# Hybrid decoder layer: last state product left out, exponential's table called early, output norm's root by Newton steps

## The chip, the cores and the metric

The kernel runs on one core of one Trainium2 chip. The metric is the device time of one execution in microseconds. Engines are TensorE (PE; PEld is its weight loads), VectorE (DVE), ScalarE (ACT), GpSimd (POOL) and SyncE (SP), which issues the weight transfers.

## The reference

One decoder layer over 512 tokens of width 1024, in float32: a SwiGLU half-step, a mixer, a second SwiGLU half-step and a final norm. The mixer projects once and runs two groups. The first is a gated DeltaNet with 4 heads of 128, in 8 chunks of 64 tokens. For each chunk:

```python
def step(state, inp):
    q_c, k_c, u_c, w_c, g_c, qk_c = inp
    v_new = u_c - w_c @ state
    o = (q_c * jnp.exp(g_c)[..., None]) @ state + qk_c @ v_new
    ...
    state = state * jnp.exp(g_last)[..., None, None] + jnp.einsum('bhcd,bhce->bhde', k_dec, v_new)
    return state, o
_, o = lax.scan(step, state0, xs)
...
o = rmsnorm(o, out_norm) * jax.nn.silu(z)
```

The state after the last chunk isn't returned. The norm divides `o` by sqrt(mean(o*o) + 1e-6), one value for each token and head. The second group is attention with 8 query heads of 64 on 2 key heads, in three branches (compressed, selected, window; at this length the selected and the window branch see all earlier keys). Both groups' outputs go through one output projection.

## The kernel before, in words

The first half-step, the projections, the mixer, the output projection and the second half-step follow each other on each engine's own queue; engines meet through semaphores only. In the mixer a list written out by `schedule()` gives all engines one order: 14 half projections, each in three groups of products (lines 592 to 594), between which come the rounds of the DeltaNet (`gdn`, a round is a list of jobs), rotary embedding and the compressed branch; then the attention's slots (`att`).

**DeltaNet.** Work is by tiles of 128 tokens (two chunks) and by pairs of tiles. `BACK` gives the four rounds of a tile's recurrence: `vn0`, `s0`, `vn1`, and `s1` with `o`. `vn` are products with the state (lines 2180, 2181), `s0` and `s1` the update's product (line 2183, 8 instructions in the trace), `o` the output product (line 2187, 16). GpSimd multiplies the state by its decay in the rounds `vn0` and `vn1` (line 2320), VectorE adds the update (line 2274), and also adds up the tile's output into `kqv` (line 2271). ScalarE copies with a scale at `vn1` (line 2206) and squares the output with a running sum at `o` (line 2219, one per head, into `t_ssq`).

**The root.** When all four tiles are squared, `dve_gdn_rms` multiplies the sums by a factor (line 2326), ScalarE takes the square root (line 2338), and `dve_gdn_fin` takes the reciprocal (2331) and the product with another factor (2333) into `t_fac`. In the schedule the first stands ahead of slot 0 of the attention, the last behind it. ScalarE's functions come from tables; a load shows as ACT_TABLE_LOAD under the line of the function that needs it. The silu of the gate z runs at the end of each of the last four half projections (line 1485).

**Attention.** There are 32 slots: each is a query tile t, a branch and a head index j, and does two heads. Tile 0 is slots 0 to 7 (128 keys), tile 1 slots 8 to 15 (256 keys), tile 2 16 to 23 (384), tile 3 24 to 31 (512). In slot i TensorE makes the scores (line 1884) and adds the mask (1887), transposes the weights of slot i - 3 (1905), and multiplies those of slot i - 4 with the values (1917). VectorE takes the scores' negated maximum (1995), for slot i - 1 the reciprocal of the sum (2001) and its product with the gate (2003), and copies half of slot i - 3's transposes (2012). ScalarE copies the other half (1963) and takes the exponentials (1971). GpSimd scales them (2045). Slot 1's scores wait for the last tile's `o`, since their banks were the DeltaNet's; the scores of slot i wait for the exponentials of slot i - 2. Behind slot 1's scores TensorE starts the output banks of two tiles with zeros and the compressed branch (lines 1934, 1937). In slots 10 to 13 VectorE scales one head of the DeltaNet's output by `t_fac` (2017); slots 23 to 26 split the first weights of the output projection; two slots past the end transpose that output (1929). Then `pe_out` projects, and its weights are loaded by SyncE as buffers come free.

Of the kernel before, what the change touches and what calls it, by code (L numbers as in the profile page):

```python
# [22 lines left out]
ACT = mybir.ActivationFunctionType  # L23
F32 = mybir.dt.float32
F32R = mybir.dt.float32r
BF16 = mybir.dt.bfloat16
AX_X = mybir.AxisListType.X
# [145 lines left out]
def gdn_rounds():  # L173

    out = []
    for p in range(PAIRS):
        t0, t1 = 2 * p, 2 * p + 1
        rounds = [[(p, "g_arg"), (p, "rb"), (p, "kk")], [], [(p, "c1")]]
        for l in range(1, 6):
            rounds += [[(p, "y%d" % l)], [(p, "t%d" % l), (p, "u%d" % l)] if l < 5 else [(p, "u5")]]  # L180
        rounds += [[(t0, "uu"), (t1, "uu")], [(p, "w0"), (p, "w1")]]
        if p == 0:
            rounds[1] += [(p, "kq"), (t0, "k_tok")]
            rounds.insert(2, [(t1, "k_tok"), (t0, "v_tok")])
            rounds[3] += [(t1, "v_tok")]
        else:
            rounds[8] += [(p, "kq")]
            rounds[9] += [(t0, "k_tok"), (t1, "k_tok")]
            rounds[10] += [(t0, "v_tok"), (t1, "v_tok")]
        if p:  # L190
            back = [[(t0 - 2, n) for n in r] for r in BACK] + [[(t0 - 1, n) for n in r] for r in BACK]
            for r, jobs in enumerate(back):
                rounds[r] = rounds[r] + jobs
        out += rounds
    back = [[(TT - 2, n) for n in r] for r in BACK] + [[(TT - 1, n) for n in r] for r in BACK]
    return out + back
# [18 lines left out]
TILE_AT = {t: n for n, t in enumerate(sorted(TILE_LAST, key=TILE_LAST.get))}  # L215
ZO_SLOT = {10 + h: h for h in range(GDN_HEADS)}
# [4 lines left out]
def schedule():  # L221
# [24 lines left out]
    out += [("gdn_rms",), ("att", 0), ("gdn_fin",)]  # L246
    return out + [("att", i) for i in range(1, NSLOT)]
# [23 lines left out]
def build(nc, dram, out):  # L271
    with ExitStack() as ctx:
# [306 lines left out]
        fin_act = sem("fin_act")  # L579
# [893 lines left out]
        def act_half_end(act, n):  # L1473
# [9 lines left out]
            if kind == "z":  # L1483
                act.wait_ge(proj_evac, CONV_EVACS + n - 3)
                act.activation(z[:, n - 10, :], z[:, n - 10, :], ACT.Silu).then_inc(z_silu, 1)

# [381 lines left out]
        def pe_attention(pe, i):  # L1868
# [4 lines left out]
            if i == 1:  # L1873
                pe.wait_ge(state_ready, 2 * TT + 1)
# [111 lines left out]
        def dve_attention(dve, i):  # L1986
# [26 lines left out]
            if i in ZO_SLOT:  # L2013
                h = ZO_SLOT[i]
                dve.wait_ge(fin_dve, 3)
# [260 lines left out]
        def pool_gdn(pool, n, name):  # L2276
# [38 lines left out]
            elif name in ("vn0", "vn1"):  # L2315
                c = int(name[2])
                pool.wait_ge(state_ready, 2 * n + c + 1)
# [6 lines left out]
        def dve_gdn_rms(dve):  # L2324
            dve.wait_ge(o_sq, 4 * TT)
            dve.tensor_tensor(tiny["vv"][:, :], tiny["ssq"][:, :], tiny["rq2"][:, :], ALU.mult)\
               .then_inc(fin_dve, 1)

        def dve_gdn_fin(dve):
            dve.wait_ge(fin_act, 1)  # L2330
            dve.reciprocal(tiny["o_rstd"][:, :], tiny["o_rms"][:, :]).then_inc(fin_dve, 1)
            dve.wait_ge(fin_dve, 2)
            dve.tensor_tensor(tiny["fac"][:, :], tiny["o_rstd"][:, :], tiny["rqs"][:, :], ALU.mult)\
               .then_inc(fin_dve, 1)

        def act_gdn_rms(act):
            act.wait_ge(fin_dve, 1)
            act.activation(tiny["o_rms"][:, :], tiny["vv"][:, :], ACT.Sqrt, scale=1.0 / GDN_DK, bias=eps_col)\
               .then_inc(fin_act, 1)

# [79 lines left out]
        def act_mixer(act):  # L2420
# [10 lines left out]
            for what, *n in SCHEDULE:  # L2431
# [9 lines left out]
                elif what == "gdn_rms":  # L2441
                    act_gdn_rms(act)
                elif what == "att":
                    act_attention(act, *n)
                elif what == "gdn":
                    for tt, name in ROUNDS[n[0]]:
                        if (tt, name) != (0, "g_arg"):
# [4 lines left out]
        def dve_mixer(dve):  # L2452
# [4 lines left out]
            for what, *n in SCHEDULE:  # L2457
# [12 lines left out]
                elif what == "gdn_rms":  # L2470
                    dve_gdn_rms(dve)
                elif what == "gdn_fin":
                    dve_gdn_fin(dve)
# [216 lines left out]
```

## Time and profile before

| | us |
|---|---|
| median of 3 runs | 1116.54 |
| lowest and highest | 1116.14, 1116.83 |
| the profiled execution | 1116.19 |
| its span in the trace | 1114.4 |
| busy: TensorE, VectorE | 1082.6, 778.0 |
| busy: ScalarE, GpSimd | 446.5, 443.5 |

Times in the trace count from the span's start. The DeltaNet and the attention share the stretch from 460 to 713 us; the edit touches 616 to 650. "Granted clock" is TensorE's clock as a share of 2.4 GHz. A busy TensorE isn't TensorE at its peak, since it also counts as busy at half its clock.

### The profile page before, as it was taken

Reading aid. Unit: us, or ns where it says so; the run is one execution under the profiler, and the core shown is the slowest. Engines: PE = TensorE matmul, PEld = TensorE weight load, DVE = VectorE, ACT = ScalarE, POOL = GpSimd, SP = SyncE. Lnnn points to the kernel's source line nnn. Section 1 sums busy time; section 2 is a strip of 40 time slices with the busy share of each in tenths; the row PEclk is TensorE's granted clock in tenths of the full one; section 3 lists DMA queues with packets and bytes.
Section 4 is the critical chain, followed back from the end, with each engine's and each line's share of the span. In section 5 each row is a group of like instructions: output and inputs, shape, how many; then the busy total and the mean of one; then the engine's idle time right before and its main releaser. Section 6 shows DMA issues by size and latency. Waiting matters only on the chain.

```text
span 1114.4 us, 20141 instructions
## 1 busy us (share of the span) xinstructions
PE 1082.6 (97%) x8484; PEld 938.2 (84%) x8484; DVE 778.0 (70%) x941; ACT 446.5 (40%) x639; POOL 443.5 (40%) x281
## 2 busy tenths in 40 slices
PE   6899999999999999999999999999999999999996
PEld 5799899988998888887787667888898899989986
DVE  5998379946987566653566487566997389837964
ACT  6534244423435334311214566343453145413432
POOL 0663169505833000312300389433480279306912
PEclk9999999999999999999999899999999999999999
DMA  6244233333232222113103001123133323422222
GB/s 228 77 124 151 76 94 99 116 108 103 89 112 95 87 103 76 40 58 134 39 28 86 4 1 39 36 79 103 59 104 115 111 77 114 135 92 80 101 85 76
DMA packets 34590, 98.45 MB, mean 88 GB/s; under 512 B 3664, under 2 KB 10320, under 8 KB 32848
## 3 DMA queue, kind: packets, MB, share of 16 engines
q1 hardware_dynamic: 34224, 97.26, 26.7%
q8 instruction: 57, 0.93, 0.3%
q14 instruction: 21, 0.17, 0.0%
q10 hardware_dynamic: 288, 0.08, 0.0%
HBM read 95.24 MB, written 2.10 MB: 87 GB/s over the span
## 4 chain that ended last, share of the span: by engine, by line
PE 87%; DVE 8%; ACT 3%; issue 2%; DMA 0%; POOL 0%; DVEq 0%; ACTq 0%
PE bank L592 25%; PE bank L594 24%; PE bank L593 24%; PE bank L2131 3%; PE bank L1917 1%; PE bank L1884 1%; PE bank L1905 1%; DVE hb_lo L716 1%; DVE w_lo L1020 1%; PE bank L2183 1%; DVE cv L1611 1%; DVE w_lo L1097 1%; PE bank L2180 1%; PE bank L1716 1%; PE bank L1520 1%
## 5 line engine op out<-in xcount | busy, mean ns | idle before, releaser
L592 PE MATMUL bank<-hb_hi,w_hi 128*128 128x256 f32 x1064 | 295.5, 278 | 6.9 <-DVE w_lo L1097 3.6
L594 PE MATMUL bank<-hb_hi,w_lo 128*128 128x256 f32 x1064 | 294.7, 277 | 0.0
L593 PE MATMUL bank<-hb_lo,w_hi 128*128 128x256 f32 x1064 | 294.7, 277 | 0.0
L592 PEld LDWEIGHTS bank<-hb_hi,w_hi 128*128 128x128 f32 x1064 | 200.5, 188 | 8.7 <-DVE w_lo L1097 4.5
L593 PEld LDWEIGHTS bank<-hb_lo,w_hi 128*128 128x128 f32 x1064 | 200.5, 188 | 0.3
L594 PEld LDWEIGHTS bank<-hb_hi,w_lo 128*128 128x128 f32 x1064 | 200.6, 189 | 0.0
L592 PE MATMUL bank<-act_hi,w_hi 128*128 128x512 f32 (+1 forms) x460 | 180.4, 392 | 10.0 <-DVE w_lo L1033 9.8
L593 PE MATMUL bank<-act_lo,w_hi 128*128 128x512 f32 (+1 forms) x460 | 179.8, 391 | 0.0
L594 PE MATMUL bank<-act_hi,w_lo 128*128 128x512 f32 (+1 forms) x460 | 179.6, 391 | 0.0
L1014 ACT ACTIVATE w_hi<-raw 128x1536 fp32r<-128x1536 f32 (+1 forms) x67 | 108.7, 1622 | 161.1 <-PE bank L594 161.1
L1020 DVE TENSOR_TENSOR w_lo<-raw,w_hi 128x1536 fp32r<-128x1536 f32 (+1 forms) x67 | 159.2, 2376 | 15.8 <-ACT w_hi L1014 15.3
L1047 POOL TENSOR_TENSOR w_sum<-raw 128x512 f32<-128x512 f32 x34 | 58.5, 1720 | 250.0 <-PE bank L594 220.1
L1097 DVE TENSOR_TENSOR w_lo<-w_sum,w_hi 128x1024 fp32r<-128x1024 f32 x76 | 114.1, 1503 | 9.4 <-POOL w_sum L1051 9.2
L1083 ACT ACTIVATE w_hi<-w_sum 128x1024 fp32r<-128x1024 f32 x76 | 80.2, 1058 | 88.4 <-POOL w_sum L1052 74.4
L592 PEld LDWEIGHTS bank<-act_hi,w_hi 128*128 128x128 f32 x460 | 87.0, 189 | 29.9 <-DVE w_lo L1033 9.8
L592 PE MATMUL bank<-h_hi,w_hi 128*128 128x512 f32 x264 | 109.9, 416 | 0.0
L594 PE MATMUL bank<-h_hi,w_lo 128*128 128x512 f32 x264 | 105.0, 398 | 0.0
L593 PE MATMUL bank<-h_lo,w_hi 128*128 128x512 f32 x264 | 105.0, 398 | 0.0
L594 PEld LDWEIGHTS bank<-act_hi,w_lo 128*128 128x128 f32 x460 | 86.9, 189 | 19.9
L593 PEld LDWEIGHTS bank<-act_lo,w_hi 128*128 128x128 f32 x460 | 86.9, 189 | 19.3
L1220 DVE SCALAR_TENSOR_TENSOR x<-bank,x 128x512 f32<-128x512 f32 x46 | 29.6, 686 | 102.2 <-PE bank L594 102.2
L1051 POOL TENSOR_TENSOR w_sum<-raw,w_sum 128x512 f32<-128x512 f32 x34 | 78.5, 2308 | 2.7
(307 smaller groups left out, 1702.6 us busy)
## 6 DMA issues: line engine op xcount, KB each, us to landing
raw<-in_gate_up SPq DMA_DIRECT2D x43, 1024.0 KB, 5.4
raw<-in_w_in SPq DMA_DIRECT2D x13, 1024.0 KB, 4.9
raw<-in_down SPq DMA_DIRECT2D x8, 1024.0 KB, 5.1
raw<-in_down SPq DMA_DIRECT2D x16, 512.0 KB, 4.1
raw<-in_down SPq DMA_DIRECT2D x8, 768.0 KB, 4.3
raw<-in_w SPq DMA_DIRECT2D x8, 512.0 KB, 3.8
x<-in_x SPq DMA_DIRECT2D x4, 512.0 KB, 7.5
raw<-in_w_out SPq DMA_DIRECT2D x4, 512.0 KB, 4.6
```

The source lines that it names most:

```text
L592: pe.matmul(out_ap, wh, xh, start=first, stop=False)
L593: pe.matmul(out_ap, wh, xl, start=False, stop=False)
L594: return pe.matmul(out_ap, wl, xh, start=False, stop=last)
L716: dve.tensor_tensor(hb_lo[:, b], HB_RAW[b], hb_hi[:, b].bitcast(F32), ALU.subtract).then_inc(hb_lo_dve, 1)
L1014: act.activation(w_hi[:, par, 0:cols], raw[:, par, 0:cols], ACT.Copy).then_inc(hi_ready, 1)
L1020: dve.tensor_tensor(w_lo[:, par, 0:cols], raw[:, par, 0:cols], w_hi[:, par, 0:cols].bitcast(F32), ALU.subtract).then_inc(lo_ready, 1)
L1047: pool.tensor_tensor(S[0], A[3], A[2], ALU.add).then_inc(s_sum, 1)
L1051: pool.tensor_tensor(S[3], A[0], S[1], ALU.subtract).then_inc(s_sum, 1)
L1083: act.activation(w_hi[:, st.step % 2, c], w_sum[:, st.step % 2, c], ACT.Copy).then_inc(s_hi, 1)
L1097: dve.tensor_tensor(w_lo[:, par, c], w_sum[:, par, c], w_hi[:, par, c].bitcast(F32), ALU.subtract).then_inc(s_lo, 1)
L1220: dve.scalar_tensor_tensor(x[:, k, :], banks[4 * (st.step % 2) + ab][:, :], 0.5, x[:, k, :], ALU.mult, ALU.add).then_inc(x_added, 1)
L2131: mm = pe.matmul(o[ch, q, :], a, b, start=True, stop=True)
```

## The change

Tile 3's last round does `o` alone: without TensorE's product `s1`, VectorE's addition, and GpSimd's decay ahead of it. Slot 1 of the attention waits for one state update less. Behind the last silu ScalarE takes the exponential of one column, which is used nowhere. The squares of the last tile move on ScalarE from the DeltaNet's last round to behind slot 1 of the attention. The square root of ScalarE and the reciprocal go. Instead `dve_gdn_root` runs behind slots 4 to 8 on VectorE, on 128 x 16 numbers: in slot 4 the mean and a first guess by integer arithmetic on the number's bits, in slots 5, 6 and 7 one Newton step each of three instructions, in slot 8 the product with the factor. Each of the 13 instructions waits for the one ahead. The stages `gdn_rms` and `gdn_fin` leave the schedule.

```diff
@@ -192,7 +193,8 @@
             for r, jobs in enumerate(back):
                 rounds[r] = rounds[r] + jobs
         out += rounds
-    back = [[(TT - 2, n) for n in r] for r in BACK] + [[(TT - 1, n) for n in r] for r in BACK]
+    last = BACK[:-1] + (["o"],)
+    back = [[(TT - 2, n) for n in r] for r in BACK] + [[(TT - 1, n) for n in r] for r in last]
     return out + back
 
 
@@ -213,6 +215,7 @@
 TILE_LAST = {t: max(i for i, a in enumerate(ATT_PAIRS) if a[0] == t) for t in range(TT)}
 TILE_ENDS = {i: t for t, i in TILE_LAST.items()}
 TILE_AT = {t: n for n, t in enumerate(sorted(TILE_LAST, key=TILE_LAST.get))}
+ROOT_SLOT, ROOT_TURNS = 4, 3
 ZO_SLOT = {10 + h: h for h in range(GDN_HEADS)}
 FAC_SLOT = {NPAIR: (0, 1), NPAIR + 1: (2, 3)}
 OG_SLOT = {NPAIR + 1: (0, 1), NPAIR + 2: (2, 3)}
@@ -243,8 +246,7 @@
     while r < len(ROUNDS):
         out.append(("gdn", r))
         r += 1
-    out += [("gdn_rms",), ("att", 0), ("gdn_fin",)]
-    return out + [("att", i) for i in range(1, NSLOT)]
+    return out + [("att", i) for i in range(NSLOT)]
 
 
 CMP_AT = {23: ("hid_sum",), 25: ("kcvc",), 26: ("scores", 0), 27: ("scores", 1), 30: ("scores", 2),
@@ -576,7 +578,6 @@
         o_ready = sem("o_ready")
         o_sq = sem("o_sq")
         fin_dve = sem("fin_dve")
-        fin_act = sem("fin_act")
         on_ready = sem("on_ready")
         o_turned = sem("o_turned")
         og_ready = sem("og_ready")
@@ -1483,6 +1484,8 @@
             if kind == "z":
                 act.wait_ge(proj_evac, CONV_EVACS + n - 3)
                 act.activation(z[:, n - 10, :], z[:, n - 10, :], ACT.Silu).then_inc(z_silu, 1)
+                if n == HALVES_N - 1:
+                    act.activation(root_first, eps_col, ACT.Exp)
 
         def dve_half_end(dve, n):
             kind, ab = HALF_KIND[n // 2], n % 2
@@ -1871,7 +1874,7 @@
                 pe.wait_ge(consts_bf, 3)
                 pe.wait_ge(proj_evac, CONV_EVACS + 10)
             if i == 1:
-                pe.wait_ge(state_ready, 2 * TT + 1)
+                pe.wait_ge(state_ready, 2 * TT)
                 pe.wait_ge(o_ready, TT)
             if i < NPAIR:
                 t, br, j = ATT_PAIRS[i]
@@ -2012,7 +2015,7 @@
                 dve.tensor_copy(p_att_t[u % 4][:, 0:n], t_bank(u)[:, 0:n]).then_inc(pt_evac_b, 1)
             if i in ZO_SLOT:
                 h = ZO_SLOT[i]
-                dve.wait_ge(fin_dve, 3)
+                dve.wait_ge(fin_dve, 4 + 3 * ROOT_TURNS)
                 o_h = kqv[:, 8 + h, :].rearrange("p (t n) -> p t n", t=TT)
                 dve.tensor_tensor(o_h, o_h, over(tiny["fac"][:, h:16:4], P), ALU.mult).then_inc(on_ready, 1)
             if i in SPLIT_SLOTS:
@@ -2314,6 +2317,8 @@
                 negated(n + 1)
             elif name in ("vn0", "vn1"):
                 c = int(name[2])
+                if (n, c) == (TT - 1, 1):
+                    return
                 pool.wait_ge(state_ready, 2 * n + c + 1)
                 pool.wait_ge(e_ready, 1)
                 at = 16 * c + 4 * n
@@ -2321,23 +2326,27 @@
                     [P, GDN_HEADS, GDN_DK]), ALU.mult).then_inc(sdec_ready, 1)
 
 
-        def dve_gdn_rms(dve):
-            dve.wait_ge(o_sq, 4 * TT)
-            dve.tensor_tensor(tiny["vv"][:, :], tiny["ssq"][:, :], tiny["rq2"][:, :], ALU.mult)\
-               .then_inc(fin_dve, 1)
-
-        def dve_gdn_fin(dve):
-            dve.wait_ge(fin_act, 1)
-            dve.reciprocal(tiny["o_rstd"][:, :], tiny["o_rms"][:, :]).then_inc(fin_dve, 1)
-            dve.wait_ge(fin_dve, 2)
-            dve.tensor_tensor(tiny["fac"][:, :], tiny["o_rstd"][:, :], tiny["rqs"][:, :], ALU.mult)\
-               .then_inc(fin_dve, 1)
-
-        def act_gdn_rms(act):
-            act.wait_ge(fin_dve, 1)
-            act.activation(tiny["o_rms"][:, :], tiny["vv"][:, :], ACT.Sqrt, scale=1.0 / GDN_DK, bias=eps_col)\
-               .then_inc(fin_act, 1)
-
+        def dve_gdn_root(dve, i):
+            ms, y, t = [tiny[n][:, :] for n in ("vv", "o_rstd", "o_rms")]
+            if i == ROOT_SLOT:
+                dve.wait_ge(o_sq, 4 * TT)
+                dve.tensor_tensor(ms, tiny["ssq"][:, :], tiny["rq2"][:, :], ALU.mult).then_inc(fin_dve, 1)
+                dve.wait_ge(fin_dve, 1)
+                dve.tensor_scalar(ms, ms, 1.0 / GDN_DK, EPS, ALU.mult, ALU.add).then_inc(fin_dve, 1)
+                dve.wait_ge(fin_dve, 2)
+                dve.tensor_scalar(y.bitcast(I32), ms.bitcast(I32), -0.5, float(0x5f3759df), ALU.mult, ALU.add)\
+                   .then_inc(fin_dve, 1)
+            elif ROOT_SLOT < i <= ROOT_SLOT + ROOT_TURNS:
+                n = 3 + 3 * (i - ROOT_SLOT - 1)
+                dve.wait_ge(fin_dve, n)
+                dve.tensor_tensor(t, y, y, ALU.mult).then_inc(fin_dve, 1)
+                dve.wait_ge(fin_dve, n + 1)
+                dve.scalar_tensor_tensor(t, t, -0.5, ms, ALU.mult, ALU.mult).then_inc(fin_dve, 1)
+                dve.wait_ge(fin_dve, n + 2)
+                dve.scalar_tensor_tensor(y, t, 1.5, y, ALU.add, ALU.mult).then_inc(fin_dve, 1)
+            elif i == ROOT_SLOT + ROOT_TURNS + 1:
+                dve.wait_ge(fin_dve, 3 + 3 * ROOT_TURNS)
+                dve.tensor_tensor(tiny["fac"][:, :], y, tiny["rqs"][:, :], ALU.mult).then_inc(fin_dve, 1)
 
         def out_bank(par, ab):
             return banks[(0, 1, 4, 5)[2 * par + ab]][:, :]
@@ -2438,13 +2447,13 @@
                     act_cmp_exp(act)
                 elif what == "cmp_pt":
                     act_cmp_pt(act, *n)
-                elif what == "gdn_rms":
-                    act_gdn_rms(act)
                 elif what == "att":
                     act_attention(act, *n)
+                    if n[0] == 1:
+                        act_gdn(act, TT - 1, "o")
                 elif what == "gdn":
                     for tt, name in ROUNDS[n[0]]:
-                        if (tt, name) != (0, "g_arg"):
+                        if (tt, name) not in ((0, "g_arg"), (TT - 1, "o")):
                             act_gdn(act, tt, name)
             act_out(act)
             act_ffn_start(act, 1)
@@ -2467,10 +2476,7 @@
                     dve_cmp_softmax(dve, *n)
                 elif what == "att":
                     dve_attention(dve, *n)
-                elif what == "gdn_rms":
-                    dve_gdn_rms(dve)
-                elif what == "gdn_fin":
-                    dve_gdn_fin(dve)
+                    dve_gdn_root(dve, *n)
                 elif what == "gdn":
                     for tt, name in ROUNDS[n[0]]:
                         if (tt, name) != (0, "g_arg"):
```

## Rows read from the trace of the kernel before

**Rows 1.** The page: TensorE's busy time, its share of the span, its instructions.

```profile
PE 1082.6 (97%) x8484; PEld 938.2 (84%) x8484; DVE 778.0 (70%) x941; ACT 446.5 (40%) x639; POOL 443.5 (40%) x281
```

**Rows 2.** The chain of waits, 621 to 632: start us, us, what.

```profile
621.60 1.08 PE bank L2183 x8
622.69 1.04 PE bank L2187 x16
...
623.75 0.70 DVE kqv L2271
...
624.48 1.28 ACT cv L2219 x8
...
625.77 1.28 ACT L2338
...
627.07 0.31 ACT t_o_rms L2338
...
627.39 1.28 ACT L1971
...
628.69 0.81 ACT p_att L1971 x4
```

**Rows 3.** Windows: stretch, length, each engine's busy us, clock, DMA share, GB/s.

```profile
628.00:631.40 3.40, 1.70 (x14) 1.07 (x14) 1.72 (x10) 3.01 (x14) 1.42 (x3) 1.00 0.00 0
631.40:641.70 10.30, 10.30 (x57) 5.83 (x56) 4.52 (x25) 4.74 (x25) 6.79 (x12) 0.50 0.01 3
641.70:655.00 13.30, 12.96 (x112) 7.32 (x112) 12.42 (x43) 10.14 (x38) 11.53 (x14) 1.00 0.01 2
```

**Rows 4.** TensorE's timeline, start of the attention: start us, us, what, [idle before].

```profile
624.59 0.49 PE L1884 MATMUL bank<-nk_rot,nq_rot 64*128 64x128 f32 x4 [0.24 <-DVE kqv L2271]
...
626.79 1.09 PE L1937 MATMUL bank<-pre,bdv 128*64 128x128 f32 x16
629.54 0.49 PE L1884 MATMUL bank<-nk_rot,nq_rot 64*128 64x128 f32 x4 [1.66 <-ACT p_att L1971]
```

**Rows 5.** VectorE's timeline, slots 2, 6, 8, 9 and 10.

```profile
630.24 0.49 DVE L1995 TENSOR_REDUCE neg_max<-bank 128x1 f32<-128x128 f32 x2 [0.35 <-PE bank L1887]
...
636.77 0.49 DVE L1995 TENSOR_REDUCE neg_max<-bank 128x1 f32<-128x128 f32 x2 [1.14 <-PE bank L1887]
...
637.45 0.29 DVE L2012 COPY p_att_t<-bank 128x128 f32<-128x128 f32 x1
...
641.42 0.76 DVE L1995 TENSOR_REDUCE neg_max<-bank 128x1 f32<-128x256 f32 x2 [1.57 <-PE bank L1887]
...
643.05 0.76 DVE L1995 TENSOR_REDUCE neg_max<-bank 128x1 f32<-128x256 f32 x2 [0.40 <-PE bank L1887]
...
644.50 0.76 DVE L1995 TENSOR_REDUCE neg_max<-bank 128x1 f32<-128x256 f32 x2 [0.21 <-PE bank L1887]
```

**Rows 6.** GpSimd's timeline: the last but two decay, the scaling of slot 5.

```profile
603.37 1.04 POOL L2320 TENSOR_TENSOR state_dec<-state,e_sums 128x512 f32<-128x512 f32 x1 [40.87 <-DVE state L2274]
...
637.63 1.18 POOL L2045 TENSOR_SCALAR h_raw<-h_raw,fgate 128x128 f32<-128x128 f32 x2 [0.93 <-DVE fgate L2003]
```

**Rows 7.** ScalarE's timeline: last silu, slot 2, a square after attention, the next load.

```profile
622.36 0.63 ACT L1485 ACTIVATE z<-z 128x512 f32<-128x512 f32 x1 [1.17 <-DVE z L1511]
...
630.56 0.37 ACT L1971 ACTIVATE h_raw<-bank,neg_max 128x128 f32<-128x128 f32 x1 [0.38 <-DVE neg_max L1995]
...
725.49 0.63 ACT L610 ACTIVATE sq<-x 128x512 f32<-128x512 f32 x1 [9.72 <-DVE x L2388]
...
763.29 1.28 ACT L676 ACT_TABLE_LOAD   x1
```

**Rows 8.** VectorE's timeline: small dependent instructions in the compressed softmax.

```profile
603.21 0.17 DVE L1840 TENSOR_SCALAR cmp_sum<-cmp_sum 128x32 f32<-128x32 f32 x1
603.42 0.35 DVE L1842 RECIPROCAL cmp_f<-cmp_sum 128x32 f32<-128x32 f32 x1
603.81 0.73 DVE L1846 TENSOR_TENSOR cmp_f<-cmp_f,sg 128x16 f32<-128x16 f32 x2
```

More of the change, by code:

```diff
@@ L26 @@
 BF16 = mybir.dt.bfloat16
+I32 = mybir.dt.int32
 AX_X = mybir.AxisListType.X
```

## The prediction

> **What bounds the kernel now.** I read the page first: TensorE is busy for 97% of the span [rows 1], so time can be saved only where it waits or runs slowly. Next I read the chain of waits around the edit. From 621.60 it leaves TensorE's weight products and runs serially: the last state product s1 (1.08 us), the output product of token tile 3 (the piece at 622.69), its addition on VectorE (0.70), ScalarE's four squares (1.28), a table load for the square root (1.28), its use (0.31), a table load for the exponential (1.28), and only then the exponentials of slots 0 and 1 at 628.69 [rows 2]. The reader should see that each link waits for the one before, and that 2.56 us of it are two table loads.
>
> The windows then show what this costs TensorE twice. Between 628.0 and 631.4 it is busy for 1.70 of 3.40 us; from 631.4 to 641.7 it is busy all the time, but at a granted clock of 0.50, that is 1.2 GHz in place of 2.4, and from 641.7 it is back at 1.00 [rows 3]. Before the fall it had done half a stretch of work, and before the rise a run of slots with 128 keys and the first with 256. In that slow stretch a slot of attention takes 2.11 us: VectorE idles 1.14 and works 0.97 (636.77 to 637.74) [rows 5], and GpSimd works 1.18 [rows 6]. After 641.7 the VectorE is busy 12.42 of 13.30 us [rows 3]: there it is the bound.
>
> **Part 1: the last state product goes.** Nobody reads the state after chunk 7. Eight matmuls (1.08 us) go from TensorE's queue, with GpSimd's decay (one instruction, off the chain) and VectorE's addition (done before the output product was). The output product moves from 622.69 to 621.60, its addition from 623.75 to 622.66, ending at about 623.36 [rows 2]. Slot 1's scores wait for that addition; they came 0.15 us after its end, at 624.59 [rows 4], and now come at 623.51. Behind them stands the start of the output banks, ending at 627.88 [rows 4] (626.79 and 1.09), 3.29 us after slot 1's start and queued ahead of slot 2's scores. So slot 2's scores can start at 626.80. Before, they waited for slot 0's exponentials until 629.54 [rows 4]. **If the exponentials are no longer late, the gain at slot 2 is 2.74 us**: 1.08 is the removed product, the rest the table and root work.
>
> **Part 2: the table.** The last silu runs 622.36 to 622.99 [rows 7]. The load follows (1.28, as in [rows 2]) to 624.27, the dummy exponential ends at about 624.5; ScalarE is otherwise idle there until 624.48. Slot 0's maxima on VectorE follow the tile's addition and are done near 623.9, so the exponentials start at about 624.4 instead of 628.69. Two slots of them take until 625.8; then the four moved squares (1.28) until 627.1. Slot 2's exponentials come 1.02 us after its scores (629.54 to 630.56) [rows 4, 7], here 627.8. So the squares cost nothing, hidden behind the output banks' start with 0.7 us to spare; without that cover they would cost up to 1.28.
>
> What the squares need of the table: ScalarE squared x at 725.49, after the attention's exponentials and before the next load, at 763.29 [rows 7]. So squares run under the exponential's table, and no load comes back.
> A load plus a further drain of about the same length is what the Trainium skill ("ScalarE: Activation LUTs", What ACT_TABLE_LOAD costs) gives for each switch, 2.66 us. Here the exponential begins 1.30 us after the load at 627.39 does [rows 2], so the trace disagrees. By the skill slot 2's exponentials would come some 0.6 us later.
>
> **Part 3: Newton steps.** VectorE gives up a reciprocal and two waits for ScalarE, and gets 13 tiny instructions: three in slot 4, three in each of 5 to 7, one in 8. Each waits for the one before. None of before has exactly this form. The near bounds: a dependent pair of 32-column instructions starts 0.21 us apart, two 16-column ones with a strided operand take 0.73, that is up to 0.40 each [rows 8]. I take 0.21, since the new operands are dense: 0.63 a slot. At 1.2 GHz this hides in the 1.14 us of idleness; with a fast TensorE it doesn't.
>
> **Part 4: the clock.** With slot 2 at 626.80 the stretch that idled is filled: slots 2 and 3 until 628.1, transposes of slot 0, slot 4 at about 628.6 (it waits for slot 2's exponentials, 0.7 us). I expect no fall. At full clock even a slot of 256 keys takes TensorE 1.45 us (maxima at 643.05 and 644.50, VectorE idle for TensorE ahead of both) [rows 5], GpSimd 1.18 at 128 keys [rows 6]. VectorE needs 0.97 less 0.08 of overlap, plus 0.63: 1.52. **VectorE becomes the bound of slots 4 to 7, at 1.5 us in place of 2.11.** Maxima follow scores by 0.70 (629.54 to 630.24) [rows 4, 5]; slot 4's start at 629.3, slot 8's four periods on at 635.3 or 635.4. Before: 641.42 [rows 5]. That is 6.1. In slots 8 and 9 VectorE idled 0.40 and 0.21 us ahead of the maxima at 643.05 and 644.50 [rows 5]; behind a full VectorE queue this mostly vanishes, while the last factor costs 0.2: about 0.4 net. **Gain: 6.5 us.**
>
> What is late next: slots 10 to 13 keep their VectorE bound (each also scales one head), then TensorE takes over. The output projection's weights are consumed and reloaded in step with the attention, and the rest is a rigid copy 6.5 us earlier. Queues of SyncE get no instruction.
>
> The profiled execution took 1116.19 us (span 1114.4), 0.35 under the median 1116.54. 1116.19 - 6.5 = 1109.7; on the median's footing 1110.0.
>
> **The rivals.**
> *Clock falls nevertheless (chance 0.15).* For it: slots of 128 keys, ten microseconds long and without a gap, didn't bring the clock back [rows 3]. Against: from 641.7 to 655 it stayed at 1.00 with gaps, and the idle half stretch is gone. Then only slot 2's gain stays: 2.74, Newton hidden, 1113.5; if the fall is shorter, between the two.
> The Trainium skill ("TensorE: Matmul & The Clock Gate", A second HAM failure mode) says that frequent short idle gaps between groups of matmuls can also make the clock swing. No gap of that kind did it here after 641.7.
>
> *VectorE pays more (0.10).* At 0.40 a step, a slot needs 0.89 + 1.20 = 2.09, nearly the old 2.11; four slots cost 2.3 more: 1112.3.
>
> *Slower (0.03): GpSimd holds VectorE up.* Newton's steps read two operands from SBUF while GpSimd scales in all of slots 4 to 8. If each of the 13 is stretched to over 0.21 + 6.5/13 = 0.71 us, the kernel is slower than before; at 1 us, 13 x 0.3 = 3.8 more than that, 1120.3. For it: the pair at 603.81 that took up to 0.40 each ran beside a GpSimd instruction (603.37 to 604.41) [rows 6, 8]. Against: that is still 0.40, not 0.71.
>
> *The edit doesn't do what it says (0.04).* If the four squares bring their own table in, two loads stand between slots 1 and 2: 1.28 x 2 + 1.28 from 625.8 gives slot 2's exponentials at 629.7 against 630.56, the gap stays and so does the slow clock: 0.9 faster, 1115.6. The square at 725.49 speaks against it.
>
> **How the numbers follow.** Forecast 0.68, own range 1108.6 to 1111.4 (step 0.15 to 0.32 us, and the ends of slots 8 and 9). About 0.2% (2.2 us) is what a measurement here can tell from no change. The range reaches over the dear VectorE and the fallen clock: 1108.4 to 1113.7. Faster by over 0.2% (under 1114.3): forecast, clock rival, dear VectorE: 0.93; same, with the useless table: 0.04; slower: 0.03.
>
> **What would show it.** Right: one table load between the last silu and slot 0; exponentials near 624.4; slot 2's scores near 626.8 with no wait for ScalarE; a granted clock of 1.00 through to 655; Newton steps 0.21 us apart; slots 4 to 7 1.5 us long; slot 9's maxima near 636.7. Wrong: a second load before the squares; a stretch at 0.50 after 628; slots over 1.7 us; or a gain at slot 9 that is gone by the output projection at 713.

## The result, and the profile after

The changed kernel took 1111.07 us in the median of 5 runs (1108.88 to 1112.52), beside 1116.54 (1115.68 to 1117.0) before. The ratio is 0.9953, with a 95% interval of 0.9936 to 0.9970. Two later sets gave 1110.56 and 1111.30, so that 21 runs have a median of 1111.10. The profiled execution took 1108.88 us, the fastest of the five; its span is 1107.1.

The page's first part, and the chain's shares by line:

```profile
PE 1077.4 (97%) x8476; PEld 936.0 (85%) x8476; DVE 778.5 (70%) x950; ACT 445.1 (40%) x638; POOL 444.3 (40%) x280
...
PE bank L593 26%; PE bank L594 25%; PE bank L595 25%; PE bank L2134 3%; PE bank L1887 1%; PE bank L1920 1%; PE bank L1908 1%; DVE cv L1614 1%; PE bank L2186 1%; PE bank L2183 1%; PE bank L1719 1%; DVE neg_max L1998 1%; PE bank L1523 1%; DVE hb_lo L717 1%; DVE w_lo L1098 1%
```

TensorE is busy for 5.2 us less than in [rows 1], though only 8 matmuls (1.08 us) went. Most of the rest is work that ran at full clock where it had run at half: in the attention (below), and near 392 and 460, where this execution, by the draw, didn't slow down.

Lines have moved by one to three: the scores are L1887, the mask L1890, the maxima L1998, the exponentials L1974. ScalarE's timeline, from the last silu to slot 2 (answers to [rows 2, 7]):

```profile
621.37 0.63 ACT L1486 ACTIVATE z<-z 128x512 f32<-128x512 f32 x1 [1.17 <-DVE z L1514]
622.02 1.28 ACT L1488 ACT_TABLE_LOAD   x1
623.31 0.20 ACT L1488 ACTIVATE root_first<-eps_col 128x1 f32<-128x1 f32 x1
623.42 0.35 ACT L1974 ACTIVATE p_att<-bank,neg_max 128x128 f32<-128x128 f32 x1
...
624.79 0.32 ACT L2222 ACTIVATE cv<-kqv 128x128 f32<-128x128 f32 x1
...
626.75 0.37 ACT L1974 ACTIVATE h_raw<-bank,neg_max 128x128 f32<-128x128 f32 x1 [0.69 <-DVE neg_max L1998]
```

There is one load behind the silu and none after it. The exponentials of slots 0 and 1 start at 623.42, that is 2.05 us behind the silu's start (before: 628.69 - 622.36 = 6.33), the squares follow at 624.79, and slot 2's exponentials at 626.75 waited for VectorE's maxima, not for the squares. TensorE's timeline (to [rows 4]):

```profile
622.51 0.49 PE L1887 MATMUL bank<-nk_rot,nq_rot 64*128 64x128 f32 x4 [0.24 <-DVE kqv L2274]
...
624.71 1.09 PE L1940 MATMUL bank<-pre,bdv 128*64 128x128 f32 x16
625.74 0.49 PE L1887 MATMUL bank<-nk_rot,nq_rot 64*128 64x128 f32 x4
...
627.61 0.49 PE L1887 MATMUL bank<-nk_rot,nq_rot 64*128 64x128 f32 x4 [0.30 <-ACT h_raw L1974]
```

Slot 2's scores at 625.74 now stand right behind the output banks' start, with no wait; before they waited 1.66 us. A wait of 0.30 us is left at slot 4. The windows, cut as in [rows 3] (columns as there):

```profile
627.10:630.50 3.40, 3.02 (x28) 1.75 (x28) 3.07 (x18) 2.79 (x17) 3.22 (x6) 1.00 0.02 5
630.50:640.80 10.30, 9.83 (x82) 5.50 (x82) 9.25 (x44) 8.24 (x35) 8.96 (x14) 1.00 0.01 2
640.80:654.00 13.20, 12.96 (x124) 8.70 (x126) 11.30 (x36) 8.82 (x32) 12.23 (x15) 1.00 0.00 1
```

The granted clock is 1.00 all through. VectorE is busy for 9.25 of 10.30 us, where it had been for 4.52. Its timeline from slot 4 to slot 10 (to [rows 5]), with the first three instructions of the root:

```profile
628.30 0.49 DVE L1998 TENSOR_REDUCE neg_max<-bank 128x1 f32<-128x128 f32 x2 [0.15 <-PE bank L1890]
...
629.18 0.23 DVE L2333 TENSOR_TENSOR t_vv<-t_ssq,t_rq 128x16 f32<-128x16 f32 x1
629.44 0.20 DVE L2335 TENSOR_SCALAR t_vv<-t_vv 128x16 f32<-128x16 f32 x1
629.68 0.30 DVE L2337 TENSOR_SCALAR t_o_rstd<-t_vv 128x16 int32<-128x16 int32 x1
629.90 0.47 DVE L1998 TENSOR_REDUCE neg_max<-bank 128x1 f32<-128x128 f32 x2
...
631.29 0.48 DVE L1998 TENSOR_REDUCE neg_max<-bank 128x1 f32<-128x128 f32 x2
...
633.04 0.48 DVE L1998 TENSOR_REDUCE neg_max<-bank 128x1 f32<-128x128 f32 x2
...
634.42 0.75 DVE L1998 TENSOR_REDUCE neg_max<-bank 128x1 f32<-128x256 f32 x2
...
635.69 0.76 DVE L1998 TENSOR_REDUCE neg_max<-bank 128x1 f32<-128x256 f32 x2
...
637.29 0.76 DVE L1998 TENSOR_REDUCE neg_max<-bank 128x1 f32<-128x256 f32 x2 [0.37 <-PE bank L1890]
```

The maxima of slots 4 to 8 start 1.60, 1.39, 1.75 and 1.38 us apart, 6.12 us in all. The first three steps of the root start 0.24 and 0.26 us apart here, the Newton steps of slots 5 to 7 0.19 to 0.24.

**How the traces are compared.** Single executions of one kernel turned out to differ by several us, so spans of single traces say little. I use two marks inside a trace: the start of the last silu on ScalarE, and the start of the last of the attention's additions into h_lo on VectorE (the one at 714.00 in the first trace of before, the one at 706.75 in that of after). Their distance is called **the stretch**: 91.64 us before, 85.38 after, 6.26 less. The remaining 1.0 us of the 7.3 between the two spans lies ahead of the silu, which starts at 622.36 and 621.37: the first execution had stretches at half clock of 3.4 us from 392.5 and from 460.8, the other had neither (but a longer one at 54). The change doesn't touch that part.

| kernel | stretch | clock in it | runs, median | ratio and interval |
|---|---|---|---|---|
| before | 91.64; 89.89 | falls; falls | 28 runs, 1116.28 | |
| last product left out | 86.59 | 1.00 | 12, 1114.27 | 0.9972 (0.9957 to 0.9987) |
| root and table only | 86.14 | 1.00 | 12, 1111.55 | 0.9957 (0.9940 to 0.9973) |
| changed | 85.38; 85.41; 85.39 | 1.00 | 21, 1111.10 | 0.9948 (0.9933 to 0.9964), third set |
| changed, no early call | 85.41 | 1.00 | 12, 1110.28 | 0.9954 (0.9939 to 0.9969) |
| changed, squares in old place | 85.42 | 1.00 | 6, 1111.08 | 0.9954 (0.9938 to 0.9971) |
| before, wait filled | 87.66; 87.64 | 1.00 | 18, 1111.87 | 0.9966 (0.9951 to 0.9981), second set |
| root early | 84.96; 84.97 | 1.00 | 21, 1110.98 | 0.9953 (0.9938 to 0.9968), first set |
| root early, DeltaNet's wait filled | 84.94 | 1.00 | 10, 1107.48 | 0.9934 (0.9912 to 0.9956) |

("Root early" is a version described below. A ratio compares all runs of one set with the runs of before taken beside them, whose medians were 1116.54, 1116.15, 1116.45 and 1116.28; it isn't the quotient of the medians. The 28 runs of before are the ones beside the third set of the changed kernel, the second sets of the filled kernel and of root early, and the last kernel.)

### The profile page after: what moved, and what is told of

It reads as the page before. It is cut to its first block, busy times and chain, and to the rows that moved or that the text cites. A ratio compares the mean times of both kernels' runs of the same rounds, so it can differ in the third digit from the quotient of the medians.

```text
span 1107.1 us, 20129 instructions
## 1 busy us (share of the span) xinstructions
PE 1077.4 (97%) x8476; PEld 936.0 (85%) x8476; DVE 778.5 (70%) x950; ACT 445.1 (40%) x638; POOL 444.3 (40%) x280
## 4 chain that ended last, share of the span: by engine, by line
PE 90%; DVE 6%; ACT 2%; issue 1%; DMA 0%; DVEq 0%; POOL 0%; ACTq 0%
PE bank L593 26%; PE bank L594 25%; PE bank L595 25%; PE bank L2134 3%; PE bank L1887 1%; PE bank L1920 1%; PE bank L1908 1%; DVE cv L1614 1%; PE bank L2186 1%; PE bank L2183 1%; PE bank L1719 1%; DVE neg_max L1998 1%; PE bank L1523 1%; DVE hb_lo L717 1%; DVE w_lo L1098 1%
```

## The experiments

### Is it the wait or the clock, and is the fall always there?

The kernel before was run again, unchanged:

> The kernel before, for a second trace. In the first its clock fell at 631.4 for 10.2 us. Theory A (the fall follows from the half idle stretch ahead of slot 2 and comes in every execution): a stretch at 0.50 of 7 to 14 us beginning between 625 and 635. Theory B (the chip looks at the engine on a clock of its own, so the same idle gap drops it in some executions and not in others; then before's times spread too): possibly no fall at all, and then slots 4 to 7 of 1.25 us and an end 4 us sooner behind the last silu.

The median was 1116.57, ratio 1.0001 (0.9988 to 1.0014), single runs from 1112.80 to 1118.29. The windows of its trace:

```profile
625.40:628.80 3.40, 1.74 (x26) 1.21 (x20) 1.41 (x8) 3.07 (x10) 0.51 (x1) 1.00 0.00 0
628.80:635.60 6.80, 6.80 (x40) 3.96 (x38) 3.62 (x21) 3.79 (x20) 5.40 (x10) 0.50 0.01 2
635.60:653.00 17.40, 17.05 (x150) 10.01 (x150) 14.95 (x54) 12.99 (x51) 15.35 (x19) 1.00 0.01 2
```

The same sequence of instructions and the same idle gap, but the fall came at 628.8 and lasted 6.8 us, against 631.4 and 10.2 us in [rows 3]. Theory A holds as far as that both traces fell. B holds as far as that the place and length vary: the stretch was 89.89 us, 1.75 us less. That is the run-to-run part of the gain, and the prediction had none.

Two traces say little of how often it falls. Each run also has a mean granted clock over its whole span; the falls outside the attention lower it too, but in the changed kernel as well as in before. Of 92 runs of before in four sets, 79 have 0.990 or less and none is over 0.993 (the first trace: 0.989, the second: 0.993). Of the changed kernel's 21, two have 0.990, the rest 0.991 to 0.994. So half-clock stretches beyond the changed kernel's are the rule in before. The second trace is one of the three highest; besides its shorter fall in the attention it also lacks those near 54 and 392, so the mean can't say which length of fall is the usual one.

Then the gap alone was filled with work that computes nothing:

```diff
+FILL = 7
...
+                if i == 2:
+                    for _ in range(FILL):
+                        pe.matmul(banks[6][:, :], zero_bf[:, :], per_head(ident_bf[:, :]), start=True,
+                                  stop=True)
                 if i >= 2:
                     pe.wait_ge(exp_done, 2 * i - 2)
```

> The kernel before with seven products of zeros (128 x 512, some 0.22 us each, 1.5 us in all) on TensorE ahead of slot 2's scores, into a bank that is overwritten later; they only fill its wait for slot 0's exponentials. Theory (the gap is what costs the clock): no fall in the attention, slots 4 to 7 at about 1.25 us in place of 2.11, the end 4 us sooner behind the last silu than in the first trace of before, and a median 2 to 4 us under that of before. Rival (products of zeros don't count, or slots of 128 keys can't hold the clock): the clock falls as in before and the time is the same, or worse by the filling.

TensorE's timeline, the filling and the scores of slots 2, 5, 6 and 7:

```profile
625.02 1.68 PE L1882 MATMUL bank<-ident_bf,zero_bf 128*128 128x512 bf16 x7
626.76 0.49 PE L1889 MATMUL bank<-nk_rot,nq_rot 64*128 64x128 f32 x4
...
630.23 0.49 PE L1889 MATMUL bank<-nk_rot,nq_rot 64*128 64x128 f32 x4
...
631.46 0.49 PE L1889 MATMUL bank<-nk_rot,nq_rot 64*128 64x128 f32 x4
...
632.69 0.49 PE L1889 MATMUL bank<-nk_rot,nq_rot 64*128 64x128 f32 x4
```

The filling took 1.68 us; the clock didn't fall, and slots 5 to 7 came 1.23 us apart with no Newton steps in the way. Slot 2's maxima stood 7.88 us behind the silu, as before (630.24 - 622.36), so up to there nothing had changed, and the stretch was 87.66 us: **the fallen clock had cost 3.98 us in the first trace of before and 2.23 in the second.** The theory holds, the rival is out. The mean granted clock of all 18 runs of this kernel (six here, twelve below) is 0.992 to 0.996, where 79 of before's 92 have 0.990 or less: so it is the wait that brings the clock down, and not only in the runs that have a trace.

The median of those six runs was 1111.14, as good as the changed kernel's. Since the stretch was 2.3 us longer I ran it again:

> The kernel before with TensorE's wait ahead of slot 2 filled, again. In its first six times it was as fast as the changed kernel (1111.1), although its trace is 2.24 us slower from the last silu to the end of the attention. Theory (six times are too few for a spread of this size): a median 2 us over that of the changed kernel in this call, 1112 to 1113.5. Rival (the filling gives something that the traces' attention doesn't show, for example fewer falls later on): again within 0.5 us of the changed kernel.

1112.71 (12 runs), beside 1111.30 for the changed kernel on the same chip, 1.4 us more where 2 had been expected; stretch 87.64. The theory's direction and its range (1112 to 1113.5) hold, and six runs had been too few. All 18 against all 21 give 0.8 us where the stretches give 2.3. The single times of both scatter by 3 to 5 us, and I can't say whether the 1.5 us between are that scatter.

The changed kernel was run twice more:

> The changed kernel once more, for a second trace and five more times. Theory (the waits around slot 2 and the slow clock from 631 to 642 are both gone, whatever the run): 5 to 7 us under the kernel before, granted clock 1.00 from slot 2 to slot 16. Rival (the clock falls in the attention in some executions, and that is why its five times spread over 3.6 us): a stretch at 0.50 between 627 and 645 in this trace, and a span nearer to 1110. A third account (the spread comes from stretches at half clock ahead of the mixer, at 54, 392 or 461): the attention looks as in the first trace, and the span differs by what lies before 620.

> The changed kernel a third time, beside the others on one chip. Theory (the spread of its times is stretches at half clock outside the attention; inside nothing varies): again 85.4 us from the last silu to the last addition of the attention and no fall between. Rival (its own clock falls there in some executions): a fall between 627 and 645.

Both traces had no fall inside the attention, and stretches of 85.41 and 85.39 us. Both fell for 3.4 us near 392 and near 460, with the last silu at 622.38 and 622.30, 1 us later than in the first. For these traces the third account holds, the rival doesn't.

### The two parts alone

Only the last state product left out of the kernel before:

```diff
-    back = [[(TT - 2, n) for n in r] for r in BACK] + [[(TT - 1, n) for n in r] for r in BACK]
+    last = BACK[:-1] + (["o"],)
+    back = [[(TT - 2, n) for n in r] for r in BACK] + [[(TT - 1, n) for n in r] for r in last]
...
-                pe.wait_ge(state_ready, 2 * TT + 1)
+                pe.wait_ge(state_ready, 2 * TT)
...
                 c = int(name[2])
+                if (n, c) == (TT - 1, 1):
+                    return
```

> The kernel before with the last state product, its decay and its addition left out, and nothing else. Theory: every link behind it moves up by 1.08 us, the wait for slot 0's exponentials and the slow clock stay: 1.1 us faster, within noise of 0.999. Rival (the chain ends at the table loads, not at the output product): no gain at all.

1114.27 beside 1116.15 before, ratio 0.9972: 1.9 us, where 1.1 was expected. Slot 2's maxima stood 6.80 us behind the silu, 1.08 less than before: the size of the part was right. But the clock (first TensorE's wait, then the windows):

```profile
628.40 0.49 PE L1885 MATMUL bank<-nk_rot,nq_rot 64*128 64x128 f32 x4 [1.66 <-ACT p_att L1972]
```

```profile
628.00:631.40 3.40, 2.75 (x22) 1.72 (x22) 2.34 (x13) 2.91 (x18) 2.56 (x5) 1.00 0.00 0
631.40:641.70 10.30, 10.30 (x93) 5.92 (x92) 8.05 (x37) 8.11 (x37) 9.48 (x15) 1.00 0.01 4
```

In this execution it didn't fall, although TensorE's wait for slot 0's exponentials was still 1.66 us; the theory had expected the slow clock to stay. The stretch was 86.59, 1.07 less than that of the filled kernel, which is the part's own worth. The 12 single times split: 1109.63 to 1112.03 in four of them and 1113.64 to 1115.27 in eight. The mean granted clocks are 0.992 to 0.994 in the four and 0.988 to 0.993 in the eight. That fits with a clock that falls in some and not in others, but only one of them has a trace, so it isn't shown.

The changed kernel with the last state product put back:

```diff
-    last = BACK[:-1] + (["o"],)
-    back = [[(TT - 2, n) for n in r] for r in BACK] + [[(TT - 1, n) for n in r] for r in last]
+    back = [[(TT - 2, n) for n in r] for r in BACK] + [[(TT - 1, n) for n in r] for r in BACK]
...
-                if (n, c) == (TT - 1, 1):
-                    return
```

> The changed kernel with the last state product put back: table, squares and Newton steps alone. Theory: slot 1's scores at their old 624.59, slot 2's scores at 627.9, the clock stays at 1.00: 5.2 to 5.6 us faster than before, that is nearly all of the gain. Rival (the gap must shrink by both parts before the clock holds): the clock falls near 631, and only 1.6 us are gained.

1111.55, ratio 0.9957; no fall, stretch 86.14. Slot 1's scores stood 2.23 us behind the silu, as before, and slot 2's 5.45, without a wait for ScalarE. Beside before's 1116.15 in the same set it gains 4.6 us, where the changed kernel (1110.56) gains 5.6: most of the gain, as the theory said, though 5.2 to 5.6 was a little too much. The rival, that both parts must shrink the gap, is out by its time: it allowed 1.6 us, and the interval of the ratio, 0.9973 at its upper end, begins at 3.0 us. One trace without a fall wouldn't do for that, since the kernel above had one too with its gap unshrunk. At a clock that holds, the root and the table are worth 87.66 - 86.14 = 1.52 us, the product 1.07, and both together 87.66 - 85.39 = 2.27, a little less than the sum.

### The early call and the place of the squares

```diff
                 act.activation(z[:, n - 10, :], z[:, n - 10, :], ACT.Silu).then_inc(z_silu, 1)
-                if n == HALVES_N - 1:
-                    act.activation(root_first, eps_col, ACT.Exp)
```

> The changed kernel without the dummy exponential behind the last silu. Theory of the prediction (the early call moves the load): without it the load stands ahead of slot 0's exponential. If a load is issued ahead of the wait of the function it serves, it starts at the same moment anyway, 0.02 us behind the silu, and slot 0's exponentials come at the same time or 0.1 us sooner: no difference. Rival (the load waits with its function for slot 0's maxima): exponentials 0.9 to 1.0 us later, slot 2's scores up to 0.3 us later, 0.3 us slower in all.

ScalarE's timeline without the call:

```profile
621.76 0.63 ACT L1486 ACTIVATE z<-z 128x512 f32<-128x512 f32 x1 [1.17 <-DVE z L1512]
622.40 1.28 ACT L1972 ACT_TABLE_LOAD   x1
623.70 0.37 ACT L1972 ACTIVATE p_att<-bank,neg_max 128x128 f32<-128x128 f32 x1
```

The load starts 0.01 us behind the silu all the same, under the line of the function it is for, though that function still has to wait for slot 0's maxima. The exponentials start 1.94 us behind the silu's start, 0.11 sooner than with the call (2.05). Stretch 85.41, median 1110.28: **the early call does nothing.** What brought the load forward is that no root, with its own table, stands between silu and exponential any more.

```diff
                     act_attention(act, *n)
-                    if n[0] == 1:
-                        act_gdn(act, TT - 1, "o")
...
-                        if (tt, name) not in ((0, "g_arg"), (TT - 1, "o")):
+                        if (tt, name) != (0, "g_arg"):
```

> The changed kernel with the four squares back in their old place, ahead of slot 0's exponentials. Theory (ScalarE has 0.7 us or more to spare until slot 2, whichever comes first): slot 0's exponentials 1.2 to 1.3 us later, slot 2's scores at the same time behind the last silu, within 0.3 us of the changed kernel at the end. Rival (the exponentials' start is what counts): 1.2 us slower at slot 2 and at the end.

With the squares ahead of slot 0 its exponentials started 3.22 us behind the silu, 1.17 later, slot 2's maxima at the same 5.05 us as in the changed kernel's second trace, and the stretch was 85.42. So the move does nothing either: ScalarE has this slack until TensorE reaches slot 2.

### A better place for the root

Here the squares stay in their old place, ahead of the load, the early call is gone, and the root's first nine instructions run in slot 1 between VectorE's maxima and the sums' reciprocal:

```diff
-ROOT_SLOT, ROOT_TURNS = 4, 3
+ROOT_SLOT, ROOT_TURNS = 1, 3
...
+            if i == 1:
+                dve_gdn_root(dve, 1)
             if 1 <= i <= NPAIR:
...
-            elif ROOT_SLOT < i <= ROOT_SLOT + ROOT_TURNS:
-                n = 3 + 3 * (i - ROOT_SLOT - 1)
+            for turn in {1: (0, 1), 6: (2,)}.get(i, ()):
+                n = 3 + 3 * turn
```

> A version that should beat both: last state product left out, squares in their old place under the silu's table, no dummy exponential, and the root's first guess with two Newton steps in slot 1 between the maxima and the sums' reciprocal (nine instructions, about 2 us, where VectorE idles 1.8 us), the third step in slot 6. Theory (nine of the Newton instructions in slots 4 to 7 cost 0.25 to 0.3 us each slot, because VectorE is the bound there): slots 4, 5 and 7 at about 1.25 us in place of 1.4 to 1.6, slot 10's maxima 0.5 to 0.9 us sooner behind the last silu than in the changed kernel, the end by as much. Rival (GpSimd or slot 2 takes over: GpSimd's first scaling comes 2 us later and its 1.18 a slot is nearly the bound): less than 0.3 us.

VectorE's timeline (the maxima of slot 1, the first and the last of the nine, the sums' reciprocal, the maxima of slots 2, 9 and 10) and ScalarE's (silu, squares, load, exponential):

```profile
625.14 0.49 DVE L1996 TENSOR_REDUCE neg_max<-bank 128x1 f32<-128x128 f32 x2 [0.44 <-PE bank L1888]
625.65 0.17 DVE L2333 TENSOR_TENSOR t_vv<-t_ssq,t_rq 128x16 f32<-128x16 f32 x1
...
627.33 0.17 DVE L2346 SCALAR_TENSOR_TENSOR t_o_rstd<-t_o_rms,t_o_rstd 128x16 f32<-128x16 f32 x1
627.77 0.17 DVE L2004 RECIPROCAL rsum<-sums 128x2 f32<-128x2 f32 x1 [0.27 <-ACT p_att L1972]
...
628.48 0.49 DVE L1996 TENSOR_REDUCE neg_max<-bank 128x1 f32<-128x128 f32 x2 [0.35 <-PE bank L1888]
...
637.32 0.76 DVE L1996 TENSOR_REDUCE neg_max<-bank 128x1 f32<-128x256 f32 x2
...
638.76 0.76 DVE L1996 TENSOR_REDUCE neg_max<-bank 128x1 f32<-128x256 f32 x2 [0.21 <-PE bank L1888]
```

```profile
623.31 0.63 ACT L1486 ACTIVATE z<-z 128x512 f32<-128x512 f32 x1 [1.17 <-DVE z L1512]
624.34 0.31 ACT L2222 ACTIVATE cv<-kqv 128x128 f32<-128x128 f32 x1 [0.40 <-DVE kqv L2274]
...
625.63 1.28 ACT L1972 ACT_TABLE_LOAD   x1
626.93 0.37 ACT L1972 ACTIVATE p_att<-bank,neg_max 128x128 f32<-128x128 f32 x1
```

The nine instructions take 1.85 us (625.65 to 627.50), 0.21 each, and end before slot 0's exponentials have released the reciprocal at 627.77. Slot 10's maxima come 15.45 us behind the silu instead of 15.92, the stretch is 84.96: 0.43 us less, just under the 0.5 to 0.9 that the theory wanted. Slots 5 and 7 last 1.24 and 1.22 us, as it said, but slot 4 lasts 1.53, as in the filled kernel, not 1.25. Slot 2's maxima are 0.11 later (TensorE now waits for slot 0's exponentials a little), and GpSimd's first scaling comes 4.92 us behind the silu instead of 3.33. The median, 1111.24, doesn't show it. Again:

> The version with the root in slots 1 and 6 again, for a second trace and more times. From its first trace: slot 10's maxima 15.45 us and the last addition of the attention 84.96 us behind the last silu, 0.45 us sooner than in the changed kernel, whatever the clock does ahead of the mixer. Median 0.4 us under the changed kernel's of the same call; the spread of single times is larger than that.

Stretch 84.97, median 1110.75, beside 1111.30 for the changed kernel in the same call. The 21 runs of both kernels have medians of 1110.98 and 1111.10. The stretch is repeatable to 0.03 us; in whole times 0.43 us can't be seen.

### Filling a wait that the change doesn't touch

The falls near 460 follow TensorE's longest wait in the DeltaNet. Its timeline in the second trace of the changed kernel, which fell there, and (last line) in the first, which didn't:

```profile
456.38 1.15 PE L2134 MATMUL bank<-kqv 128*64 128x64 f32 x32
460.18 0.91 PE L2173 MATMUL bank<-consts,kqv 128*128 128x128 f32 x4 [2.64 <-DVE lt L2242]
...
460.70 0.66 PE L2173 MATMUL bank<-consts,kqv 128*128 128x128 f32 x4 [2.64 <-DVE lt L2242]
```

To the last kernel, five products go into that wait:

```diff
             o_acc = h4(7)
+            if name == "k_tok" and tt == 0:
+                pe.wait_ge(e_ready, 1)
+                for _ in range(5):
+                    pe.matmul(banks[7][:, 256:512], ident, const("cos")[:, 0:256], start=True, stop=True)
             gdn_bank_free(pe, tt, name)
```

> The version with the root in slots 1 and 6, plus five products of 128 x 256 float32 (some 0.43 us each, 2.1 us in all) that fill TensorE's 2.64 us wait ahead of the first transposes of the DeltaNet, near 457.5, into half a bank that nobody reads afterwards. Theory (that wait costs a stretch of 3.4 us at half clock in most traces): no fall near 460, and the first transposes are at full clock; about 1.5 us sooner at the last silu in executions that would have fallen, so a median 1 to 2 us under that of the version without the filling, and 6.5 to 8 us under before. Rival (the falls ahead of the mixer are where they are for other reasons, or the filling delays the transposes): no better than 1111.

```profile
456.18 2.43 PE L2159 MATMUL bank<-consts 128*128 128x256 f32 x10
458.89 0.66 PE L2177 MATMUL bank<-consts,kqv 128*128 128x128 f32 x4 [0.28 <-DVE lt L2246]
```

The wait fell from 2.64 to 0.28 us. In this execution there was no half-clock stretch anywhere up to 1100, and the last silu started at 619.56. That alone doesn't show what the filling does: with the wait unfilled 10 of 13 traces fell near 460, but three didn't (changed, first trace; before filled, first trace; squares in the old place). The times are the better evidence. The median was 1107.48, ratio 0.9934: 8.8 us under before and 3.3 under the same kernel without the filling (1110.75 in the same set). Eight of its ten runs took less than 1109 us, and one of the nine beside it; the mean granted clocks are 0.993 to 0.998 against 0.991 to 0.996. The theory's 1 to 2 us was too low. This trace had no fall near 392 either, which the filling at 457 doesn't reach, nor one at 54. The four traces without a fall near 392 and near 460 have the silu at 619.56 to 621.37 (the later two with 6.8 us at half clock at 54), the eight with both at 622.05 to 623.76. So part of the 3.3 us may be luck, and how much is not shown: 10 runs, 1106.43 to 1116.20. It is the fastest version of the study.

## Why the prediction was right, point by point

- **Forecast 1110.0, own range 1108.6 to 1111.4.** Measured 1111.07, faster by 0.5%, in the likeliest case. The gain of the medians is 5.2 to 5.6 us where 6.5 was forecast, so the mechanism came out and the number lies near the range's upper end.
- **Part 1, 1.08 us.** Right: 1.08 at slot 2, 1.07 in the stretch.
- **Slot 2 gains 2.74 us.** Measured behind the silu: maxima at 7.88 before, 5.06 after, 2.82.
- **Part 2.** The times were right (exponentials at 624.4 forecast, 624.41 when the silu's start is put at 622.36; squares hidden with 0.7 us to spare; slot 2's exponentials waited for the maxima after 0.69 us of idleness). Its cause was not: the prediction let the early call bring the load forward. Without the call the load comes at the same time. And the squares' move, rightly priced at nothing, wasn't needed.
- **The Trainium skill's figure of a load.** Load to exponential took 1.29 us (622.02 to 623.31), again without the further drain that "ScalarE: Activation LUTs" (What ACT_TABLE_LOAD costs) adds; the trace disagrees.
- **Part 3, 0.21 us a step.** 0.24 and 0.26 for the first ones in slot 4, 0.19 to 0.24 in slots 5 to 7, both beside a busy GpSimd, and 0.21 in slot 1 of the early version, where GpSimd was idle. The dear row of 0.40 was no guide.
- **Part 4, VectorE's bound in slots 4 to 7 at 1.5 us.** 6.12 us for the four, against 6.0 forecast. Without Newton steps and at full clock they took 5.44 (filled before), so the root costs 0.68 there. Only the account by slots was too simple: slot 4 lasts 1.53 us even without them (TensorE waits for GpSimd), and slot 6 with them 1.75, where the transposes again waited 0.31 us for GpSimd.
- **Gain at slot 10, 6.5 us.** 22.14 - 15.92 = 6.22 behind the silu. At slot 8 it was 19.06 - 13.05 = 6.01 (6.1 forecast); the net 0.4 us that slots 8 and 9 were to give back was 0.21.
- **What the sum left out.** It was made against one execution, and the slow clock in it was taken as what every execution of before pays. It lasted 10.2 us in that one and 6.8 in the next. Against the second, the stretch gains 4.51 us, not 6.26. The prediction weighed that the clock might fall in the kernel after; that its fall in the kernel before is itself a draw stood in none of its cases. That the forecast hit is in part luck: made from an execution whose attention went like the second one's, the gain would have been some 1.75 us smaller (91.64 - 89.89). Why the medians gain 0.9 to 1.3 us less than forecast is shown only in part: 0.3 us is missing by slot 10, the rest isn't located.
- **A price on two footings.** The clock rival's 1113.5 is 1116.19 - 2.74; on the median's footing, as the forecast has it, it would be 1113.8.
- **The rivals.** No fall of the clock in the attention in any of nine traces with the new root, nor in the two with the wait filled. VectorE wasn't dear, GpSimd didn't hold it up, and no table came back.

## What to carry to other kernels

Where TensorE waits in the midst of small products, as here for 1.66 us, look at the granted clock of the microseconds behind it before pricing the wait, and in more than one execution: here the wait's own removal was worth 1.5 us and the clock 2 to 4, and seven products of zeros in the wait bought the clock alone. A load of ScalarE's table needs no early call, only that no function of another table stands between; the squares between silu and exponential brought none. And where single runs scatter, compare traces by the distance of two marks around the edit: 0.03 us repeatable here where the clock held between them, against several us for the whole.

## What the hardware did that I had not expected

- The same idle gap at the same place brought the clock down at 631.4 for 10.2 us in one execution and at 628.8 for 6.8 us in another, and a gap of the same 1.66 us (last product left out) not at all. "TensorE: Matmul & The Clock Gate" (What's actually happening) in the Trainium skill says that the chip watches the engine by a window that runs freely and isn't reset when a kernel starts. The differing places and lengths fit with that; no run here shows the window itself.
- Whole times scatter: 28 runs of before lie between 1112.77 and 1121.34 us, where the five first ones spanned 1.3 us. The clock is only a part of it: the slowest of the 28 has a mean granted clock of 0.989, while the ten at 0.986 took 1116.34 to 1118.68 us. What else slows some executions has no trace.
- Near 392 the clock fell in several traces without any idle time of TensorE that the timeline would show: just ahead of it stand 16 products with one column each, which count as 1.95 us busy (389.51 in the changed kernel's second trace). Whether they are the cause wasn't tried.
